# Large experts: the transposes of the first half of the activations one weight piece later in TensorE's order

## What is computed

```
def expert_block(args):
    xb, e = args
    gu = xb @ w_gu[e] + b_gu[e]
    glu = jnp.minimum(gu[:, :EXPERT_DIM], SWIGLU_LIMIT)
    lin = jnp.clip(gu[:, EXPERT_DIM:], -SWIGLU_LIMIT, SWIGLU_LIMIT)
    act = glu * jax.nn.sigmoid(SWIGLU_ALPHA * glu) * (lin + 1.0)
    return act @ w_dn[e] + b_dn[e]
```

## Time and profile before

| | |
|---|---|
| Median of 3 runs | 2680.16 us (2680.11 to 2680.64) |
| Profiled execution | 2671.66 us, of which its span 2669.7 us, and 2.0 us around it |
| TensorE busy in the span | 2377.2 us (89%) |
| VectorE busy | 1889.5 us (71%) |
| ScalarE busy | 1411.6 us (53%) |
| GpSimd busy | 537.3 us (20%) |
| Moved by DMA | 517.03 MB |

### The profile page before, as it was taken

One profiled execution on the slowest core, in us unless ns is written; L12 is line 12 of the kernel. 1 busy time (PEld: TensorE's weight loads), 2 busy tenths in 40 slices (PEclk: granted clock), 3 DMA queues, 4 the chain that ended last, 5 costly groups with the idle time before them and its releaser, 6 DMA issues.

```text
span 2669.7 us, 33681 instructions
## 1 busy us (share of the span) xinstructions
PE 2377.2 (89%) x11328; PEld 1958.3 (73%) x11328; DVE 1889.5 (71%) x2167; ACT 1411.6 (53%) x1553; POOL 537.3 (20%) x481
## 2 busy tenths in 40 slices
PE   6689998858979519999999999999999999999994
PEld 4477887747868518778778788778778778777773
DVE  3589999524333427887887887887887887787885
ACT  3452223656532115665665665665665665665665
POOL 1006884740020040110110110110110110110110
PEclk9899998759989659999999999999999999999997
DMA  5011211010023136877877877877877877877887
GB/s 132 8 39 33 56 48 40 16 71 1 1 75 119 44 124 235 297 274 261 297 274 262 300 273 262 299 273 261 301 271 264 299 273 265 294 272 261 298 285 287
DMA packets 248329, 517.03 MB, mean 194 GB/s; under 512 B 33782, under 2 KB 58454, under 8 KB 247914
## 3 DMA queue, kind: packets, MB, share of 16 engines
q1 hardware_dynamic: 234746, 470.62, 49.5%
q0 software_dynamic: 13408, 45.49, 6.5%
q10 hardware_dynamic: 112, 0.10, 0.0%
HBM read 479.95 MB, written 37.88 MB: 194 GB/s over the span
## 4 chain that ended last, share of the span: by engine, by line
PE 61%; DVE 10%; DMA 9%; ACT 6%; issue 5%; SPq 5%; POOL 3%; DVEq 0%; ACTq 0%; POOLq 0%
PE ps L1659 9%; PE ps L1661 9%; PE ps L1660 9%; DMA e_raw<-in_w_gate_up_dram 8%; PE ps L1375 6%; PE ps L1377 5%; PE ps L1376 5%; PE ps L1665 3%; PE ps L1666 3%; DVE e_wlo L2125 3%; PE ps L1554 2%; PE ps L1669 2%; SPq L702 2%; POOL tok_d L879 1%; PE ps L1545 1%
## 5 line engine op out<-in xcount | busy, mean ns | idle before, releaser
L2125 DVE TENSOR_TENSOR e_wlo<-e_raw,e_whi 128x2048 fp32r<-128x2048 f32 x398 | 901.5, 2282 | 211.0 <-ACT e_whi L1247 211.0
L1247 ACT ACTIVATE e_whi<-e_raw 128x2048 fp32r<-128x2048 f32 x399 | 756.9, 1912 | 445.6 <-PE ps L1666 196.1
L1659 PE MATMUL ps<-e_whi,xh 128*128 128x512 f32 x1056 | 417.1, 395 | 2.3 <-DVE e_wlo L2125 1.1
L1661 PE MATMUL ps<-e_wlo,xh 128*128 128x512 f32 x1056 | 412.9, 391 | 0.0
L1660 PE MATMUL ps<-e_whi,xl 128*128 128x512 f32 x1056 | 412.7, 391 | 0.0
L913 POOL DMA_INDIRECT x_d<-ym,scur x33 | 68.1, 2063 | 1023.1 <-ACT ym L1291 1004.2
L1659 PEld LDWEIGHTS ps<-e_whi,xh 128*128 128x128 f32 x1056 | 198.9, 188 | 49.6 <-issue 9.2
L1661 PEld LDWEIGHTS ps<-e_wlo,xh 128*128 128x128 f32 x1056 | 198.8, 188 | 42.4
L1660 PEld LDWEIGHTS ps<-e_whi,xl 128*128 128x128 f32 x1056 | 198.9, 188 | 40.4
L1659 PE MATMUL ps<-e_whi,ath 128*128 128x512 f32 x528 | 211.9, 401 | 17.6 <-DVE atl L2158 16.9
L1661 PE MATMUL ps<-e_wlo,ath 128*128 128x512 f32 x528 | 206.2, 391 | 0.0
(11 more groups left out here) (347 smaller groups left out, 4131.4 us busy)
## 6 DMA issues: line engine op xcount, KB each, us to landing
e_raw<-in_w_gate_up_dram SPq DMA_DIRECT2D x267, 1024.0 KB, 5.2
e_raw<-in_w_down_dram SPq DMA_DIRECT2D x132, 1024.0 KB, 6.9
w_raw<-in_w_in_dram SPq DMA_DIRECT2D x20, 512.0 KB, 3.6
xt<-in_x_dram SPq DMA_DIRECT2D x8, 512.0 KB, 3.3
wo_raw<-in_w_out_dram SPq DMA_DIRECT2D x8, 512.0 KB, 6.4
xr<-in_x_dram SPq DMA_DIRECT2D x8, 512.0 KB, 4.6
x_d<-x SPq DMA_DIRECT2D x8, 512.0 KB, 2.6
h_d<-h SPq DMA_DIRECT2D x8, 512.0 KB, 2.9
```

Source lines behind the costliest of these rows:

```text
L1247: nc.scalar.activation(e_whi[:, m % HRING, :], e_raw[:, m % RING, :], ACT.Copy).then_inc(s.e_hi, 1)
L1659: nc.tensor.matmul(dst, a_hi, slot_hi, start=False, stop=False, skip_group_check=True)
L1661: return nc.tensor.matmul(dst, a_hi, slot_lo, start=False, stop=last, skip_group_check=True)
L2125: nc.vector.tensor_tensor(e_wlo[:, m % RING, :], e_raw[:, m % RING, :], e_whi[:, m % HRING, :].bitcast(F32), ALU.subtract).then_inc(s.e_lo, 1)
```

## The change

In TensorE's list, a_transposes for half 0 is called after piece 6 instead of after piece 5 in units of kind "L". In "S" and "X" it stays after piece 5. No other engine's list is touched, and no instruction is added or removed.

```
@@ -1753,7 +1753,7 @@
                         pe.wait_ge(s.ld_xo, v.nth(16, 16))
                         x_transposes(2)
                         xo_transposes()
-                    if p == 5:
+                    if p == (6 if u.kind == "L" else 5):
                         if u.kind == "L":
                             pe.wait_ge(s.e_xl, u.nth(1, 2))
                         a_transposes(u, v, 0)
```

## The result

The changed kernel takes 2712.42 us in the median of 4 runs (2709.86 to 2714.39), the kernel before 2680.14 (2676.45 to 2680.64). The ratio is 1.0123, 95% interval 1.0105 to 1.0140: **1.2% or 32 us slower**. The forecast was 2703 us with a range of 2694 to 2710. The sign and the new wait came out as forecast, and the time lies 2.4 us above the range. The profiled execution is one of 2714.39 us, the longest of the four, its span 2712.4.

What follows compares the result with a forecast made beforehand. TensorE was taken to bound the experts. New waits of +39.7 us, restarts of +1.6 and the removed wait of -16.9 gave +24.4; a unit-by-unit count gave +23, which was taken: 2703 us, range 2694 to 2710.

Steps and rivals of the forecast that it cites:

- The wait that goes: TensorE's wait for `ao` ahead of its transposes in large units disappears: minus 16.9 us in all.
- The block behind `ath`: VectorE's dense work from `atl` to `um` in large units, 7.07 us, now starts only after the later transposes and `ath`.
- t: The new start of the transposes in a large unit, 4.98 us later than before; later steps are timed from it.
- The new wait: In piece 8 of every large unit, TensorE's overflow bias waits 2.48 us for the `uo` addition: +39.7 us in all.
- The 0.1 us for a restart: Slower matmuls just after the wait in piece 8 of each large unit: 0.1 us per unit, +1.6 us in all.
- What is queued behind: Later work on ScalarE, SyncE's loads, GpSimd's gathers and the small unit: costed at nothing.
- Rivals 1, 2 and 4: No new wait, 2663 us (0.05); small unit's `atl` wait shrinks, 2688 us (0.08); waits cancel or nothing moves, 2680 us (0.03).
- The clock: TensorE's clock among the experts stays full despite the new wait in large units: no cost in the sum.
- rival 3: TensorE's clock falls after each new wait in large units: 1.7 us per unit, 27 us more, 2730 us; chance 0.05.

Runs made afterwards that it cites:

- the two fillings: The changed kernel with eight or four unused bias matmuls per large unit ahead of the wait for the `uo` addition: 2695.07 us and 2697.41 us.
- e2: The changed kernel with VectorE's gate of half 1 and lo 8 ahead of at_lo 0 and ao_lo 0 in large units: 2663.87 us, ratio 0.9949.
- e5: The changed kernel with four unused bias matmuls per large unit ahead of the wait for the `uo` addition: 2697.41 us, ratio 1.0077.
- e6: The kernel before with only the transposes of `ao` moved after piece 6 in large units, those of `am` left after piece 5: 2690.92 us, ratio 1.0037.
- e11: The changed kernel with VectorE's gate and lo 8 first, and ScalarE's hi 9 ahead of at_hi 0, ao_hi 0 and fold_g 1: 2658.54 us, ratio 0.9933.
- e10: The changed kernel with VectorE's gate of half 1 and lo 8 first in large units, run again on another occasion: 2660.53 us, ratio 0.9944.

## Why the prediction was right and where it was wrong

- **The wait that goes.** Forecast: all 16.9 us of it. Right: the row is gone, and with VectorE's lists mended the kernel gains 13 to 18 us, so that wait was worth about what its row says.
- **The block behind `ath`.** Forecast: `atl` at t + 1.26, 7.07 us of block, `uo` done at t + 11.07. With t = 1852.33 the rows after give 1.27, 7.00 and 10.99. Right.
- **The new wait.** Forecast: 2.48 us between t + 8.74 and t + 11.22. Measured: 2.28 us between t + 8.76 and t + 11.04. The size was off by 0.2 us, half of it in the hand-over: I took 0.15 us from `ao` to its transposes, and from `uo` to the bias it was 0.05. Over 16 units it is 3 us too many. The 0.1 us for a restart came out right. Moving the gate (minus 0.6 us in the wait), adding 0.8 us (plus 0.8) and taking 2.25 us out of the block (no wait) show that the block sets it.
- **What is queued behind.** Forecast: nothing, on ScalarE, SyncE, GpSimd and in the small unit. Right: the small unit's wait is 15.0 us after 15.1, and the loads cause none. Rivals 1, 2 and 4 did not come true for the change as made.
- **The clock.** This step failed. It said "So I take the clock as staying full in the sum", because TensorE is busy around the wait, and gave rival 3 a chance of 0.05. The clock fell behind the new wait in 10 of 16 large units, in 12 the second time, at 1.6 us each, 16 to 19 us. The rival's price (1.7 us) was about right, its chance was not, and it counted on all units or none. With the wait filled and no fall the kernel takes 20 us more than before, which is 2700 us and inside the range; with the falls it is 2712. The nearest rows that I had, showed waits of 2.2 us in a stretch with a clock of 0.72. The argument from TensorE's busy share set them aside with no row that bore it out. The experts of the kernel before hold one longer wait than the table, which ends at 2605 us: 1.84 us for `atl` in the last unit. The clock stayed full behind it there, and fell behind the same wait in other runs (below). The Trainium skill's sentence (TensorE: Matmul & The Clock Gate, "HAM oscillation — how this bites in real kernels") pointed the right way, and the trace agrees with it in 10 of 16 units: there the wait throttled the array again. It did not do so each time.

That the time adds up from these terms is worked out, by 37 us in the profiled executions against 32 in the medians; that the falls come from the idle time is shown by the two fillings.

## What to carry to other kernels

When a step is moved later to hide its wait, follow its results down the hand-written lists of the other engines and write both sides of every meeting point as a time after the moved step; here 5 us of delay met a point with 0.24 us of slack. Move the work that stands behind it in those lists ahead as well: the same move with two calls of VectorE and one of ScalarE reordered turns 1.2% slower into 0.7% faster. And price a new wait of TensorE of two microseconds twice, once as idle time and once as slow matmuls behind it.

## What was not expected of the hardware

The clock's fall is no simple matter of how long one wait is. In piece 8 of the large units it fell behind none of 16 waits of 1.2 us, of 1.5 us and of 1.7 us, behind 10 and 12 of 16 of 2.1 us, and behind 9 of 16 of 2.9 us. It also fell behind 2 waits of 1.6 us that stand between two groups of small transposes. Every one of the 13 profiles has a wait of 1.8 us for `atl` in the last unit, after the loop of 16 rounds, and the clock fell behind it in four of them: `e2`, `e5`, `e6` and `e11`. In the 5 us behind it the granted clock is 0.66 in `e2` and 1.00 in `e10`, the same kernel. So for waits from 1.6 to 2.9 us these runs show both, falls and none. Which units are hit changes between executions of one kernel, and what decides between them stays open.
